# One convolution chunk and its weight unit placed before the attention steps of a two-block fp32 kernel

## What is computed

```
proj = h @ w_in                                   # 1024 -> 13 pieces, sc_b ... cfm_in
y_a = sc_b * depthwise_conv(sc_c * sc_h, w3)      # short convolution
y_b = rms_norm(gla_scan(q, k, v, la_f) + flip(gla_scan(flip...))) * silu(gg)   # gated linear attention
q_c, k_c, v_c = from rms_norm(cq) @ w_mla_uq, rms_norm(ckv) @ w_mla_ukv, rope
y_c = softmax(q_c k_c^T * scale) v_c              # 4 heads, 4 blocks of 128 queries
a, gate = split(cfm_in)
u = depthwise_conv(a * sigmoid(gate), w31)        # conformer branch, 31 taps
y_d = silu(layer_norm(u))
y = concat(rms_norm(each) * gain) @ w_out
h = layer_norm(alpha * h + y)
```

## Time and profile before

| | us |
|---|---|
| median of 3 runs | 3128.26 |
| lowest, highest | 3127.58, 3128.99 |
| the profiled execution | 3129.29 |
| its span in the profile | 3127.1 |
| TensorE busy in the span | 2864.3 |
| VectorE busy in the span | 1807.5 |
| ScalarE busy in the span | 1431.0 |
| GpSimd busy in the span | 1089.3 |

### The profile page before, as it was taken

How to read it: one execution, slowest core, us unless ns; L and a number is a source line. 1 busy time by engine, 2 the same in 40 slices (tenths; PEclk the granted TensorE clock), 3 DMA queues, 4 the chain that set the end, 5 groups by cost and what they waited for, 6 DMA issues and landing times.

```text
span 3127.1 us, 45397 instructions
## 1 busy us (share of the span) xinstructions
PE 2864.3 (92%) x13488; PEld 2314.8 (74%) x13488; DVE 1807.5 (58%) x2649; ACT 1431.0 (46%) x2025; POOL 1089.3 (35%) x643
## 2 busy tenths in 40 slices
PE   6888999998889999999999987999499999969994
PEld 5666888886668888877877866887368777758883
DVE  4876444135684442167654248998567643279996
ACT  4525455225343554212445135887212453238883
POOL 2313344543213444635643521110356444501101
PEclk9999999999999999999999998999699999979996
DMA  4212233432113333534321347999334222459993
GB/s 125 61 35 87 88 94 97 158 105 66 46 48 95 100 94 116 184 90 108 102 71 53 98 163 272 411 411 350 120 104 115 77 61 82 141 180 411 411 411 153
DMA packets 375356, 468.59 MB, mean 150 GB/s; under 512 B 31050, under 2 KB 277916, under 8 KB 375132
## 3 DMA queue, kind: packets, MB, share of 16 engines
q1 hardware_dynamic: 349568, 391.52, 37.1%
q0 software_dynamic: 14688, 53.48, 4.5%
q10 hardware_dynamic: 10876, 20.91, 2.3%
HBM read 423.09 MB, written 35.65 MB: 147 GB/s over the span
## 4 chain that ended last, share of the span: by engine, by line
PE 48%; issue 33%; POOL 12%; DVE 3%; ACT 2%; DMA 1%; ACTq 1%; POOLq 0%; SPq 0%; DVEq 0%
POOL unit_lo L411 10%; PE bank L491 7%; PE bank L492 6%; PE bank L2055 4%; PE bank L2198 4%; PE bank L2202 4%; PE bank L2199 4%; PE bank L806 2%; PE bank L2212 2%; PE bank L2216 2%; PE bank L2213 2%; PE bank L906 1%; PE bank L907 1%; PE bank L909 1%; PE bank L2128 1%
## 5 line engine op out<-in xcount | busy, mean ns | idle before, releaser
L411 POOL TENSOR_TENSOR unit_lo<-unit_raw,unit_hi 128x1024 fp32r<-128x1024 f32 (+2 forms) x194 | 465.2, 2401 | 865.6 <-ACT unit_hi L404 865.4
L491 PE MATMUL bank<-xT_hi,unit_hi 128*128 128x512 f32 (+1 forms) x1776 | 697.2, 396 | 12.1 <-issue 4.3
L492 PE MATMUL bank<-xT_lo,unit_hi 128*128 128x512 f32 (+1 forms) x1776 | 674.8, 383 | 0.0
L491 PEld LDWEIGHTS bank<-xT_hi,unit_hi 128*128 128x128 f32 x1776 | 341.7, 192 | 100.7 <-issue 31.4
L492 PEld LDWEIGHTS bank<-xT_lo,unit_hi 128*128 128x128 f32 x1776 | 341.9, 193 | 65.2 <-issue 6.0
L404 ACT ACTIVATE unit_hi<-unit_raw 128x1024 fp32r<-128x1024 f32 (+2 forms) x194 | 203.0, 1047 | 383.0 <-PE bank L806 152.7
L396 POOL TENSOR_TENSOR unit_lo<-unit_raw,unit_hi 128x1024 fp32r<-128x1024 f32 (+2 forms) x154 | 317.2, 2060 | 12.9
L394 POOL TENSOR_SCALAR unit_hi<-unit_raw 128x1024 fp32r<-128x1024 f32 (+2 forms) x154 | 145.8, 947 | 465.5 <-PE bank L2055 267.9
L476 DVE TENSOR_TENSOR wt_lo<-wt,wt_hi 128x1024 fp32r<-128x1024 f32 x192 | 229.2, 1223 | 27.6 <-ACT wt_hi L471 26.8
L476 DVE TENSOR_TENSOR xT_lo<-wt,xT_hi 128x1024 fp32r<-128x1024 f32 x192 | 234.5, 1223 | 12.5 <-ACT xT_hi L471 2.6
L806 PE MATMUL bank<-xT_hi,unit_lo 128*128 128x512 f32 x976 | 241.2, 389 | 0.0
(11 more groups left out here) (523 smaller groups left out, 6180.3 us busy)
## 6 DMA issues: line engine op xcount, KB each, us to landing
wt<-in_w SPq DMA_DIRECT2D x384, 512.0 KB, 8.5
unit_raw<-in_w_in SPq DMA_DIRECT2D x272, 256.0 KB, 3.1
unit_raw<-in_w_ffn_up SPq DMA_DIRECT2D x176, 256.0 KB, 3.1
unit_raw<-in_w_ffn_down SPq DMA_DIRECT2D x88, 256.0 KB, 3.1
unit_raw<-in_w_out SPq DMA_DIRECT2D x64, 256.0 KB, 2.9
y_rows<-yb POOLq DMA_DIRECT2D x30, 512.0 KB, 7.1
y_rows<-zeros POOLq DMA_DIRECT2D x24, 512.0 KB, 5.2
unit_raw<-in_w_br SPq DMA_DIRECT2D x96, 128.0 KB, 2.3
```

Of the source, the lines that this page charges most:

```text
L411: pool.eng.tensor_tensor(lo, raw, hi.bitcast(F32), SUB).then_inc(self.split, 1)
L491: pe.matmul(out, wh, xh, start=first, stop=False)
L492: pe.matmul(out, wh, xl, start=False, stop=False)
```

## The change

Chunk 8 takes unit 10, the values units 11 to 14; the chunks from 9 on keep units 15 to 21. In `BEGUN` chunk 8 goes to the front. TensorE takes its six pieces before the step loop, so before the first score; ScalarE evicts it before its loop. `FILL1` gets 60 pieces instead of 66; the pieces done by the end of each step are now 10, 14, 18, 22, 25, 28, 32, 35, 38, 42, 45, 48, 52, 55, 58, 61, 64, 66.

```
-        U_UQ, U_UKV, U_GV, U_OUT, U_UP, U_DOWN = 6, 8, 10, 22, 30, 74
-        U_OF = [0, 1, 2, 3, 4, 5, 7, 9] + list(range(14, 22))
+        U_UQ, U_UKV, U_GV, U_OUT, U_UP, U_DOWN = 6, 8, 11, 22, 30, 74
+        U_OF = [0, 1, 2, 3, 4, 5, 7, 9, 10] + list(range(15, 22))
...
-        FILL1 = [4, 4, 4, 4, 3, 3] + [4, 4, 3] * 4
-        BEGUN = [("gv", j, 4) for j in range(4)] + [("chunk", k, 6) for k in range(8, 14)] + [("mean", 0, 1), ("chunk", 14, 6), ("var", 0, 1), ("chunk", 15, 6)]
+        AHEAD, FILL1 = 6, [4, 4, 4, 4, 3, 3] + [4, 3, 3] * 3 + [3, 3, 2]
+        BEGUN = [("chunk", 8, 6)] + [("gv", j, 4) for j in range(4)] + [("chunk", k, 6) for k in range(9, 14)] + [("mean", 0, 1), ("chunk", 14, 6), ("var", 0, 1), ("chunk", 15, 6)]
...
             dense = dense_work()
+            for _ in range(AHEAD):
+                next(dense)
             for n in range(18):
...
-            pieces = ended = 0
+            pieces, ended = AHEAD, 1
+            evicted(8)
             for n in range(17):
```

## The result

| | median, us | ratio to before, 95% interval |
|---|---|---|
| before, beside the changed kernel | 3128.62 | |
| changed | 3149.02 (3146.19 to 3150.37) | 1.0063 (1.005 to 1.0075) |

A forecast was written before the change was run, and what follows sets the result against it. The stage was taken as bound by TensorE in some steps and VectorE in others. Terms 2.1 + 1.9 + 5.0 + 1.0 - 0.3 gave +9.7 us a layer, 19.4 in two, on 3128.3: 3147.7 us, range 3135 to 3157.

The forecast's parts named there:

- T(9): Start of the four transposes of probabilities 9, with which step 10 begins; predicted +2.1 us a layer up to there.
- the variance: Moves from step 16 to 15, where it waits for ScalarE's squares: +1.0 us a layer (0 to +1.5).
- step 11's subtraction: Chunk 12's unit's GpSimd subtraction moves onto step 11's masks and six taps: T(12) +1.9 us, 0 if it misses.
- C: End of VectorE's last conformer taps, its work of step 12, for which the mean waits.
- the mean: Moves from step 14 to 13, waits for the last tap, delays output 6: +5.0 us a layer (+3.5 to +7.2).
- T(15) to the next matmul: Tail after step 15, on VectorE and ScalarE, to the first matmul after the stage: -0.3 us a layer.
- Chunk 8 fills the hole and gives nothing: Before the first score: fills TensorE's 5.66 us idleness, worth 1.5 us at best; T(0) 0.5 us later with the subtraction.
- The subtraction lands on the gate sums: Unit 12's GpSimd subtraction falls on VectorE's gate sums before T(0), costing VectorE about 2 us.
- (b): Rival: moved subtractions hit nothing, mean at full clock; +1.3 us a layer, 3131 us, no measurable change; chance 0.13.
- (a): Rival: TensorE sets the pace everywhere, filled hole is pure gain; 6.9 us a layer, 3114.5 us; chance 0.07.
- (d): Rival: forecast plus low clock in steps 2, 13, 14 and another subtraction on taps; 13.9 us a layer, 3156; chance 0.18.

The follow-up runs named there:

- narrowed run: GpSimd's subtraction for units 12 to 21 cut to 64 of 1024 columns: kernel before 3109.97 us, changed kernel 3121.06 us.
- re-spreading: Fewer pieces in steps TensorE bounds, more where it waits: changed kernel with chunk 8 ahead 3117.55 us, kernel before with nothing moved ahead 3118.89 us.

## Why the prediction was right

The forecast was 3148, the measurement 3149, and by the same steps. That they agree to 1 us is partly luck: up to T(9) the forecast is 0.9 and 1.0 us a layer too high, for the variance in layer 2 it is 1.7 too low, and the four executions lie 4 us apart. Shift of the changed kernel against the one before, in us from the swap ahead of the stage:

| term | predicted | layer 1 | layer 2 |
|---|---|---|---|
| up to T(9) | +2.1 | +1.2 | +1.1 |
| T(9) to T(12), step 11's subtraction | +1.9 | +1.9 | +1.6 |
| T(12) to C | 0 | +0.2 | +0.1 |
| C to T(14), the mean | +5.0 | +4.8 | +4.8 |
| T(14) to T(15), the variance | +1.0 | +1.1 | +2.7 |
| T(15) to the next matmul | -0.3 | -0.5 | -0.5 |
| sum | +9.7 | +8.7 | +9.8 |

**Chunk 8 fills the hole and gives nothing.** Right: the score is at the full clock, 1.02 instead of 2.07 us, and T(0) is 0.66 us later, where 0.5 was written. The runs back the reason: with the subtractions narrowed T(0) was 2.1 us earlier, 1.4 ahead of the kernel before, which is the 1.5 that the prediction allowed the filled hole. So the hole was worth something, and the moved subtraction took it and 0.7 more.

**The subtraction lands on the gate sums.** Right in size (2.2 us), though it met the four scans and not the `tensor_tensor` behind them, which kept its 0.69 us; and the Trainium skill's rule for two SBUF inputs (SBUF — State Buffer, "Who interferes with whom"), which no row of before could show for a scan, is borne out here: 3.53 instead of 1.37 us. Without this collision rival (b) would have had its first term, as the narrowed run shows.

**T(9).** Mis-sized by 0.9 to 1.0: I took the middle between a clock drop in step 2 and none, and in layer 1 TensorE waited only 0.90 us there, not 3, since it had lost 1.7 us to half clock (granted 0.50) between T(0) and T(1) already. That loss itself cost nothing, since T(2) stands 33.0 us behind the swap in both layers, with and without it: VectorE sets it. The bound without a drop has a slip, too: +2.4 and -0.9 make 1.5, not 1.3 (measured in layer 1: +2.1 and -0.9). Layer 2 waited 2.60 us before T(2) and did drop (T(2) to T(3) took 9.3 us instead of 7.7), yet the second layer of before had a drop of its own in step 5 (7.5 us instead of 5.8), which hid it. That the two layers agree at T(9) is therefore chance.

**The mean.** Right in mechanism and size: a wait of 7.1 us (8 written), output 6 read at C + 7.6 (7.2), T(14) at C + 16.6 (16.3 to 16.8), the mean at half clock for 3.42 us (2.9 taken, 3.6 the bound), and from the reading of output 6 to the next maximum VectorE needed 5.2 us, as written, with the subtraction gone that cost it 2.0 there before. Moving only the mean in the kernel before cost some 10 us, and exchanging it with chunk 14 in the changed one gave some 10 back.

**The variance.** Written 1.0, measured 1.1 and 2.7. Moved alone in the kernel before it showed the same, +1.5 and +3.2 us from T(14) to T(15), so where that step ran at the full clock its price is above my bound of 1.5. In the first layer of before T(14) to T(15) ran partly at half clock (granted 0.63 from 239.4 to 244), which hid it: the row I subtracted from, 7.46 us, is 5.79 in the second layer. A term read off one layer where the other was to be had was the weak step.

**The rivals.** (a), filling the hole as pure gain, fell: the changed kernel is slower than the one before at full width and with the subtractions narrowed, and re-spreading gave the same time with chunk 8 ahead and without. (b) needed the subtractions to miss and the mean to be cheap; neither held. (d) needed low clocks in steps 2, 13 and 14; only the mean's, in step 13, was there in both layers.

## What to carry to other kernels

Work taken out of a filler list moves every later item forward, so look up what each item that crosses a step waits for: here one reduction that depends on another engine's last instruction, put one step too early ahead of short products in TensorE's queue, cost half of the whole loss. A hole in TensorE's timeline is worth only the time by which TensorE came later than everything else that the next step waits for (here 1.5 of its 5.7 us), what the filling sets off on other engines can cost more (here 2.1), and the pieces belong in the steps where it stands idle before another engine. Here that re-spreading alone gave some 10 us, with or without the move.

## What the runs showed that I had not expected

Keeping TensorE fed in step 10 shortened that step by 3 us, though VectorE sets when its attention product can start: behind 4.6 us of idleness the products and scores had run at half clock (1.94 us for a product that takes 1.08 when the wait is 0.92). A TensorE wait on another engine's chain is thus not free here: what comes after it stood on the same chain and ran at 1.2 GHz instead of 2.4. Nor is the length of the wait all that counts: almost the same wait before T(0) was followed by half clock in the first layer of the changed kernel (1.99 us, then four transposes in 1.12) and by the full one in the second (1.98 us, then 0.66).
